# Two RWKV directions prepared side by side, and inverse roots taken on a few columns, in a two-layer mixer network

## The reference, cut to what matters

```python
kk = heads(k * k_k)
kk = kk * lax.rsqrt(jnp.sum(kk * kk, axis=-1, keepdims=True) + 1e-12)
for d in range(2):
    log_w = -jax.nn.softplus(-(w0[d] + jnp.tanh(wd) @ w2[d])) - 0.5
    decay = jnp.exp(-jnp.exp(log_w))
    a = jax.nn.sigmoid(a0[d] + ad @ a2[d])
    g = jax.nn.sigmoid(gd) @ g2[d]
    kd = heads(k * (1.0 + (a - 1.0) * k_a))
# S_t = S_{t-1}(diag(w_t) + z_t b_t^T) + v_t k_t^T, y_t = S_t r_t, in both directions
for (_, kd, _, g), yd in zip(per_dir, y_dirs):
    bonus = jnp.sum(rh * kd * r_k, axis=-1, keepdims=True) * vh
    outs.append((_head_norm(yd, gn_g, gn_b) + bonus) * g)
out = outs[0] + outs[1]
```

## Time and profile before

| | us |
|---|---|
| median of 3 runs | 3255.99 (3255.82 to 3256.31) |
| profiled execution, device time | 3254.52 |
| its span in the trace | 3252.7 |
| mean granted TensorE clock, share of full speed | 0.948 |

### The profile page before, as it was taken

How to read it: one execution, slowest core, us unless ns; L and a number is a source line. 1 busy time by engine, 2 the same in 40 slices (tenths; PEclk the granted TensorE clock), 3 DMA queues, 4 the chain that set the end, 5 groups by cost and what they waited for, 6 DMA issues and landing times. The chain is left out here.

```text
span 3252.7 us, 55368 instructions
## 1 busy us (share of the span) xinstructions
PE 2899.6 (89%) x23162; PEld 2478.3 (76%) x23162; DVE 2074.0 (64%) x2342; ACT 1553.3 (48%) x1802; POOL 44.2 (1%) x12
## 2 busy tenths in 40 slices
PE   6995796899998985968999999999999769997899
PEld 3872684799998853966877878778788649996799
DVE  2345655554445356656888888888888556665666
ACT  2234222443344242235766766767677434452553
POOL 0200000000000100000000000000000000000000
PEclk9997898999999997978999999999999889998999
DMA  6210464255454200007988989889799314542253
GB/s 264 104 65 7 157 223 144 77 182 181 168 187 162 91 33 1 4 1 294 368 309 309 372 307 351 321 306 371 307 348 372 133 52 156 182 169 80 108 191 117
DMA packets 86193, 616.02 MB, mean 189 GB/s; under 512 B 9592, under 2 KB 11264, under 8 KB 12032
## 3 DMA queue, kind: packets, MB, share of 16 engines
q1 hardware_dynamic: 82656, 601.92, 49.5%
q10 hardware_dynamic: 3360, 11.50, 1.0%
HBM read 612.33 MB, written 1.05 MB: 189 GB/s over the span
## 5 line engine op out<-in xcount | busy, mean ns | idle before, releaser
L2126 DVE TENSOR_TENSOR ring_split<-ring,arena_split 128x2048 fp32r<-128x2048 f32 x336 | 769.2, 2292 | 114.0 <-ACT arena_split L2056 103.1
L2056 ACT ACTIVATE arena_split<-ring 128x2048 fp32r<-128x2048 f32 x336 | 645.2, 1924 | 45.8 <-PE banks L1991 45.8
L305 DVE TENSOR_TENSOR ring_split<-ring,arena_split 128x2048 fp32r<-128x2048 f32 x174 | 405.4, 2332 | 360.1 <-ACT arena_split L299 360.1
L1970 PE MATMUL banks<-arena_split 128*128 128x512 f32 x1792 | 608.4, 402 | 11.6 <-DVE ring_split L2126 11.6
L1970 PEld LDWEIGHTS banks<-arena_split 128*128 128x128 f32 x1792 | 342.1, 191 | 87.7 <-DVE ring_split L2126 14.0
L299 ACT ACTIVATE arena_split<-ring 128x2048 fp32r<-128x2048 f32 x174 | 331.9, 1910 | 153.8 <-PE banks L971 54.7
L937 PE MATMUL banks<-mix_split,ring_split 128*128 128x256 f32 x1408 | 397.8, 283 | 0.0
L937 PE MATMUL banks<-mix_split,arena_split 128*128 128x256 f32 x1408 | 393.6, 280 | 2.0 <-DVE ring_split L305 1.6
L937 PE MATMUL banks<-h_split,arena_split 128*128 128x256 f32 x1408 | 395.1, 281 | 0.0
L1970 PE MATMUL banks<-ring_split,arena_split 128*128 128x512 f32 x896 | 356.5, 398 | 0.0
L636 PE MATMUL banks<-h_split,arena_split 128*128 128x256 f32 (+1 forms) x848 | 289.4, 341 | 59.4 <-DVE mix_split L452 59.4
(11 more groups left out here) (302 smaller groups left out, 4357.8 us busy)
## 6 DMA issues: line engine op xcount, KB each, us to landing
ring<-parts SPq DMA_DIRECT2D x574, 1024.0 KB, 4.8
arena<-bias ACTq DMA_DIRECT2D x2, 2048.0 KB, 8.9
x_buf<-xt ACTq DMA_DIRECT2D x1, 2048.0 KB, 23.9
constants<-con ACTq DMA_DIRECT2D x1, 2025.0 KB, 12.7
out<-x_buf ACTq DMA_DIRECT2D x1, 1024.0 KB, 4.8
arena<-lora ACTq DMA_DIRECT2D x2, 256.0 KB, 2.7
arena<-gate ACTq DMA_DIRECT2D x2, 256.0 KB, 2.9
arena<-sgw ACTq DMA_DIRECT2D x2, 256.0 KB
```

The lines of the kernel that those rows point to most:

```text
L305: dve.tensor_tensor(low_slots[:, n % RING, :], slots[:, n % RING, :], high[:, m % high.shape[1], :].bitcast(F32), ALU.subtract).then_inc(w ...
L1970: mm = pe.matmul(pair_bank(U), x[:, k, :], w[:, j, :], start=k == 0 and g == 0, stop=k == KT - 1 and g == 2)
L2056: act.activation(high[:, m % 3, :], slots[:, m % RING, :], ACT.Copy).then_inc(wh_ok.h, 1)
L2126: dve.tensor_tensor(low_slots[:, m % RING, :], slots[:, m % RING, :], high[:, m % 3, :].bitcast(F32), ALU.subtract).then_inc(wl_ok.h, 1)
```

## The change

In the preparation the head sums of `kk`, squared on DVE, are taken with the data as weights and two columns of `head_sum` as the moving operand: 128 tokens land on partitions, and the sums of 4 heads by 512 tokens are 16 columns. Root and inverse are taken on these 16 columns. PE puts the inverses back over each head's 64 features: a column, broadcast to 128x64, is the weight and the identity the moving operand (`over_head`). Both directions have buffers of their own, and ACT takes all sigmoids first (tanh as a sigmoid of twice the argument, with a DVE step behind it), then one root, then all exponentials. The factor on the log decays goes into the exponentials' scale; the exclusive decay is the inclusive one read a token earlier; the key scale runs on ACT. The bonus product is stored, and its head sum, the product with v and the gate stand behind the loop, on the needed tokens only. The layer norm of the convolution and the group norm take their inverse roots on few columns in the same way; the group norm goes q = 0, 2, 1, 3, with gain and gate fused into two DVE operations. Layer 1 leaves out the output half of `zr` and of its products for chunks that are not needed.

The diff, without the table of step names and most removed lines (they stand above):

```diff
...
+        head_cols = C("head_sum").rearrange("p (h f) -> p h f", h=2)[:, :, 0]
+        over_head = lambda a: a.broadcast_to((P, DH))
+        hs = [slice(0, DH), slice(DH, 2 * DH)]
...
+            pe.wait_ge(V_.h, V_.at("sq"))
+            for i in range(8):
+                hp, b = divmod(i, 4)
+                mm = pe.matmul(bank(7)[:, 2 * i:2 * i + 2], kd[:, hp, b * P:(b + 1) * P], head_cols, start=True, stop=True)
             mm.then_inc(P_.h, P_.one("kksum"))
...
+            pe.wait_ge(A_.h, A_.at("sw11"))
+            pe.wait_ge(V_.h, V_.at("inv"))
+            for i in range(8):
+                hp, b = divmod(i, 4)
+                for j, h in enumerate(hs):
+                    mm = pe.matmul(INV(hp)[h, b * P:(b + 1) * P], over_head(kk_inv[:, 2 * i + j:2 * i + j + 1]), C("ident"),
+                                   start=True, stop=True)
+            mm.then_inc(P_.h, P_.one("kkinv"))
...
+                act.activation(tw[0:64, d, :], us[0:64, 6 + 2 * d, :], ACT.Sigmoid, scale=2.0).then_inc(A_.h, A_.one(f"tanh{d}"))
+            for d in range(2):
+                act.activation(sgd[:, d, :], us[:, 7 + 2 * d, :], ACT.Sigmoid).then_inc(A_.h, A_.one(f"sgd{d}"))
...
+            def decays(d):
+                act.wait_ge(V_.h, V_.at(("scan10", "first")[d]))
+                act.activation(ep[d], en[d], ACT.Exp, scale=rate).then_inc(A_.h, A_.one(f"ep{d}"))
...
+                act.activation(en[d], en[d], ACT.Exp, scale=-rate).then_inc(A_.h, A_.one(f"en{d}"))
+            act.wait_ge(P_.h, P_.at("kksum"))
+            key_scale(0)
+            act.wait_ge(V_.h, V_.at("kkc"))
+            act.activation(kk_root, kk_root, ACT.Sqrt, bias=eps(EPS_KK)).then_inc(A_.h, A_.one("root"))
+            decays(0)
+            decays(1)
+            act.wait_ge(V_.h, V_.at("k0"))
+            key_scale(1)
...
+            own()
+            mult(kd, kk, kk, "sq")
+            for d in range(2):
+                dve.wait_ge(A_.h, A_.at(f"tanh{d}"))
+                dve.tensor_scalar(tw[0:64, d, :], tw[0:64, d, :], 2.0, -1.0, ALU.mult, ALU.add).then_inc(V_.h, V_.one(f"tw{d}"))
+            dve.wait_ge(P_.h, P_.at("kksum"))
+            dve.tensor_copy(kk_root, bank(7)[:, 0:16]).then_inc(V_.h, V_.one("kkc"))
+            for d in range(2):
...
+            own()
...
+            dve.wait_ge(A_.h, A_.at("root"))
+            dve.reciprocal(kk_inv, kk_root).then_inc(V_.h, V_.one("inv"))
+            def keys(d):
+                dve.wait_ge(A_.h, A_.at(f"ka1{d}"))
+                mult(kd, kd, k, f"kd{d}")
+                own()
+                for hp in range(2):
+                    dve.scalar_tensor_tensor(bonus[d][:, hp, c0:T], r[:, hp, c0:T], Q1(l, "r_k", hp), kd[:, hp, c0:T],
+                                             ALU.mult, ALU.mult).then_inc(V_.h, V_.one(f"rk{hp}{d}"))
+            def rows(d):
...
+                dve.wait_ge(P_.h, P_.at("kkinv"))
+                for hp in range(2):
+                    dve.scalar_tensor_tensor(zr[:, 2 * d + hp, :, 0, inner], e[:, hp, :, moved], -1.0, kc[:, hp, :, inner],
+                                             ALU.mult, ALU.mult).then_inc(V_.h, V_.one(f"z{hp}{d}"))
+                for hp in range(2):
+                    dve.tensor_scalar(zr[:, 2 * d + hp, :, 0, edge], kc[:, hp, :, edge], -1.0, None, ALU.mult)\
+                        .then_inc(V_.h, V_.one(f"e{hp}{d}"))
...
+            def columns(d):
+                own()
+                mult(bt[:, 2 * d:2 * d + 2, :], kk, av[d], f"b1{d}")
+                dve.wait_ge(A_.h, A_.at(f"en{d}"))
+                mult(kt[:, 2 * d:2 * d + 2, :], kd, en[d], f"k{d}")
+                own()
+                mult(bt[:, 2 * d:2 * d + 2, :], bt[:, 2 * d:2 * d + 2, :], en[d], f"b{d}")
             for d in range(2):
+                keys(d)
+                if not d:
+                    dve.wait_ge(P_.h, P_.at("kkinv"))
+                    for hp in range(2):
+                        mult(kk[:, hp, :], kk[:, hp, :], INV(hp), f"kkn{hp}")
+                    own()
+                rows(d)
+                columns(d)
...
+                    rows = 2 if seen(g) else 1
...
+                        mm = pe.matmul(bank(b)[h, q * 128:q * 128 + rows * CH], keys[h, q, c * CH:(c + 1) * CH], z_r[h],
...
+                if not j:
+                    for hp in range(2):
+                        mm = pe.matmul(bank(hp)[:, 0:n], C("head_sum"), bonus[0][:, hp, c0:T], start=True, stop=True)
+                    mm.then_inc(bnP.h, bnP.one("s0"))
+                    pe.matmul(bank(2)[:, 0:n], C("head_sum"), bonus[1][:, 0, c0:T], start=True, stop=True)\
+                        .then_inc(bnP.h, bnP.one("s1"))
                 fill_pe(pe, NG, f"u{j}")
...
+                if not j:
+                    pe.wait_ge(cvA.h, cvA.at("sq1"))
+                    for b in range(cv_n // P):
+                        for i in range(2):
+                            mm = pe.matmul(bank(4)[:, b:b + 1], cv_sq[:, i, b * P:(b + 1) * P], C("mean_cv")[:, 0:1],
...
+                    mm.then_inc(cvP.h, cvP.one("var"))
+                else:
+                    pe.wait_ge(cvV.h, cvV.at("inv"))
+                    for b in range(cv_n // P):
+                        mm = pe.matmul(bank(3)[:, b * P:(b + 1) * P], cv_inv[:, b:b + 1].broadcast_to((P, P)), C("ident"),
+                                       start=True, stop=True)
+                    mm.then_inc(cvP.h, cvP.one("inv"))
                 fill_pe(pe, NG, f"dx{j}")
...
+                    pe.wait_ge(bnV.h, bnV.at("v00"))
+                    pe.matmul(bank(0)[:, 0:n], C("head_sum"), bonus[1][:, 1, c0:T], start=True, stop=True)\
+                        .then_inc(bnP.h, bnP.one("s2"))
...
+                if j:
+                    dve.wait_ge(cvA.h, cvA.at("root"))
+                    dve.reciprocal(cv_inv[:, 0:cv_n // P], cv_root[:, 0:cv_n // P]).then_inc(cvV.h, cvV.one("inv"))
...
+                for hp in range(2):
+                    dve.wait_ge(bnP.h, bnP.at("s0" if not j else f"s{1 + hp}"))
...
+                    dve.tensor_tensor(bonus[j][:, hp, c0:T], sums, v[:, hp, c0:T], ALU.mult).then_inc(bnV.h, bnV.one(f"v{hp}{j}"))
+            dve.wait_ge(cvP.h, cvP.at("inv"))
...
+                dve.tensor_tensor(flat(acc[i]), flat(acc[i]), bank(3)[:, 0:cv_n], ALU.mult).then_inc(cvV.h, cvV.one(f"n{i}"))
...
+            dve.wait_ge(bnV.h, bnV.at("v11"))
+            for d in range(2):
+                for hp in range(2):
+                    o = bonus[d][:, hp, c0:T]
+                    dve.tensor_tensor(o, o, gg[:, 2 * d + hp, c0:T], ALU.mult).then_inc(bnV.h, bnV.one(f"g{hp}{d}"))
...
+            dve.tensor_tensor(bon[:, :, c0:T], bon[:, :, c0:T], bonus[1][:, :, c0:T], ALU.add).then_inc(bnV.h, bnV.one("add"))
...
+        order = (0, 2, 1, 3)
...
+            def var(q):
+                pe.wait_ge(A_.h, A_.at(f"s{q}"))
+                for b in range(nb):
+                    mm = pe.matmul(bank(4 + q)[:, 2 * b:2 * b + 2], sq[:, q, b * P:(b + 1) * P], head_cols, start=True, stop=True)
+                mm.then_inc(P_.h, P_.one(f"v{q}"))
+            def expand(q):
+                pe.wait_ge(V_.h, V_.at(f"i{q}"))
+                for b in range(nb):
+                    for j, h in enumerate(hs):
+                        mm = pe.matmul(bank(q)[h, b * P:(b + 1) * P], over_head(gn_inv[:, q, 2 * b + j:2 * b + j + 1]), C("ident"),
+                                       start=True, stop=True)
+                mm.then_inc(P_.h, P_.one(f"e{q}"))
...
+            for i in range(1, 4):
...
+            act.activation(warm, eps(EPS_RMS), ACT.Sqrt).then_inc(S("root_ready").h, S("root_ready").one())
...
+            for i in range(1, 4):
...
+            def invert(q):
+                dve.wait_ge(A_.h, A_.at(f"r{q}"))
+                dve.reciprocal(gn_inv[:, q, 0:2 * nb], gn_root[:, q, 0:2 * nb]).then_inc(V_.h, V_.one(f"i{q}"))
+            def gain(q):
+                dve.wait_ge(P_.h, P_.at(f"e{q}"))
+                dve.scalar_tensor_tensor(dv[:, q, :], dv[:, q, :], Q1(l, "gn_g", q % 2), bank(q)[:, 0:n], ALU.mult, ALU.mult)\
+                    .then_inc(V_.h, V_.one(f"g{q}"))
+            def gated(q):
+                own()
+                dve.scalar_tensor_tensor(dv[:, q, :], dv[:, q, :], Q1(l, "gn_b", q % 2), gg[:, q, c0:T], ALU.add, ALU.mult)\
+                    .then_inc(V_.h, V_.one(f"b{q}"))
...
+            invert(0)
+            own()
+                gain(hp)
+                invert(2 + hp)
+                gated(hp)
+                own()
+                dve.tensor_tensor(dv[:, hp, :], dv[:, hp, :], bon[:, hp, c0:T], ALU.add).then_inc(V_.h, V_.one(f"add{hp}"))
+                gain(2 + hp)
+                if not hp:
+                    invert(1)
+                gated(2 + hp)
+                own()
+                dve.tensor_tensor(mixT[:, 4 + hp, c0:T], dv[:, hp, :], dv[:, 2 + hp, :], ALU.add).then_inc(V_.h, V_.one(f"o{hp}"))
```

267 lines of the change are left out of this document (113 added, 154 removed).

## The result

The changed kernel takes 3183.7 us (median of four, 3179.3 to 3189.8) against 3255.9 for the kernel before (3254.5 to 3256.3): a ratio of 0.978, 95% interval 0.977 to 0.979. Five more executions beside later experiments gave 3182.4 against 3254.9, ratio 0.978 (0.976 to 0.979). The forecast was 3178, with 3168 to 3198 as the range. The profiled execution is the slowest of the four, 3189.8 us with a span of 3188.0; a second one, profiled later, took 3181.3 (span 3179.5).

What follows compares the result with a forecast made beforehand. PE was taken to bound most of the program, but DVE chains four stretches of 183 us. From 3254.5 us, savings in preparations, second loop and group norms less 5.8 lost gave 3176.4, with 1.5 to the median 3178; range 3168 to 3198.

Steps and rivals of the forecast that it cites:

- preparation, layer 0: Preparation of layer 0: a chain through DVE ending at 36.9 instead of 65.9 us, 29.0 us saved.
- preparation, layer 1: Preparation of layer 1: the same chain with half the tokens for r and bonus, 34.3 of 63.8 us, 29.5 saved.
- loop, layer 0: End of the first loop: last chunk 3.9 us later and 1.9 more on DVE behind it, 5.8 us lost.
- loop, layer 1: Second loop: fewer product columns and half masks save 2.8, its end loses 0.6 to 1; 2.2 us saved.
- group norm, layer 0: Group norm of layer 0: DVE-led behind the first expansion, 17.6 of 33.0 us, 15.4 saved.
- group norm, layer 1: Group norm of layer 1, half as wide: 12.5 of 20.3 us, 7.8 saved.
- rival 2: Each of the 160 expansion instructions pays its weight load: +9 to +17 us, about 3190; chance 0.06.
- rival 3: All 276 new small products run one by one, 0.33 us more each, 91 us: 3269; chance 0.02.
- Rival 4: Loop's end grows another 8 to 10 us as modulation pieces, ACT's copies and bonus wait in turn: 3187; chance 0.06.
- rival 1: PE's clock does not come up in preparations and group norms: about +18 us, 3196; chance 0.12.
- the first 5.3 us: Start of layer 0's group norm: mean products with the clock coming up, expected to stay at 5.3 us.
- DVE waits for no expansion after the first: Expected sign in the profile: group norms of 17.6 and 12.5 us, DVE waiting for no expansion but the first.

Runs made afterwards that it cites:

- experiment 2: Changed kernel with the key norms' inverse root back at full width, in DVE's idle gap ahead of the scans, without expansion: 3186.0 us (+3.6).
- experiment 6: Changed kernel with layer 1's key products against z and r back to both rows for every chunk: 3185.4 us (+2.9).
- Experiment 8: Changed kernel with products nobody reads put on PE where it idles, in the preparations and at the loop ends: 3169.4 us (-13.0).
- experiment 5: Changed kernel with the whole bonus term moved from the loop's end back into the preparation: 3183.9 us (+1.5).
- experiment 3: Changed kernel with the group norm alone back to wide sums, roots and inverses: 3202.3 us (+19.9).
- experiment 4: Changed kernel with the convolution's layer norm alone back to full width, without expansion: 3190.2 us (+7.8).
- experiment 1: The changed kernel again, with no edit: 3182.4 us (3181.3 to 3184.2).

## Why the prediction was right, and where its terms were off

By its own steps; the second profile stands behind the first, since the first has the dip:

| step | forecast | first profile | second |
|---|---|---|---|
| preparation, layer 0 | -29.0 | -27.30 | -27.70 |
| preparation, layer 1 | -29.5 | -28.85 | -28.85 |
| loop, layer 0 | +5.8 | +8.50 | +5.80 |
| loop, layer 1 | -2.2 | -1.80 | -1.95 |
| group norm, layer 0 | -15.4 | -12.85 | -13.25 |
| group norm, layer 1 | -7.8 | -7.20 | -7.00 |
| sum | -78.1 | -69.50 | -72.95 |

**The mechanism was right.** Four chains through DVE end where their phases end; 72.5 us between the medians stand against 73.0 in the windows of the second profile. The price of the expansion instructions, for which no row stood, holds: 16 in 1.09 us at full clock, 32 in 3.5 to 3.7 at half (0.055 and 0.107 apart beyond the finish of the last), so rivals 2 and 3 are out. The Trainium skill (TensorE: Matmul & The Clock Gate, Part 3: Packing small matmuls) lets a weight load overlap running products, in its list of what overlaps, only where the row group differs (its paragraph on the mechanism also allows a load into the background weight buffer); here every instruction uses all 128 rows, and the 0.055 and 0.107 leave no room for an exposed load. The trace disagrees with the rule of the list. The first out_project phase does not wait for weights: ACT starts it 0.2 us behind the group norm's end.

**The end of the first loop** is the term I had expected to be least sure, and in the second profile it is exact (+5.8; tail 28.4 against 22.8 before). Its two parts hold as well: from the mean product to the last chunk 4.2 us more (forecast 3.9), behind that 1.4 more (forecast 1.9). Rival 4, another 8 to 10 us, did not come. The first profile's +8.5 is 2.7 above the sum, by the dip of the clock and not by waits of PE, ACT and bonus for each other.

**What was mis-sized is the clock in short phases,** 4.9 us in all: rival 1 in a mild form. In the first preparation the low-rank products were to run at full clock after 4 us of work and did so after 8.8: 1.3 us in the phase. My 4 us came from a stretch with products of 512 columns only, and experiment 2, with such a head sum, needed 5. The step that failed is counting the 2-column head sum towards it in the same way. In the group norm I kept "the first 5.3 us"; they became 6.2 to 6.6, where the phase starts after 4.2 us of idle PE instead of 3.6, and its last expansions fell back to half clock, so the row "DVE waits for no expansion after the first" is wrong (0.5 and 0.6 us): 2.1 us. In the second group norm everything behind the means ran at half clock: 0.8. (That one has no fixed size: unaltered, it took 11.2 and 10.5 us in experiments 2 and 6, less than my 12.5.) The preparation of layer 1 lacks 0.7 for the same kind. Experiment 8 bears the clock out as the cause: it changes only what keeps PE busy, and these four windows are then 34.1, 33.2, 16.0 and 10.2 us, below my 36.9, 34.3, 17.6 and 12.5. It doesn't show that no smaller error of another kind hides in them.

**Two attributions inside a right sum were wrong.** I booked 6.6 us for the wide inverses; experiment 2 puts them back in another place for 0.3 and 1.0. And 12.7 for the bonus; experiment 5 shows 6.2 of it to be work that is merely done elsewhere. The removed sum was right because it was read from the whole phase, but neither number is what the edit is worth by itself. The group norm (20.8 us, experiment 3) and the convolution's layer norm (5.2 in windows, experiment 4) are worth what DVE's rows say, since nothing covers them.

What stays open: what causes the dip in the first loop's tail. It is in 8 of 12 profiles that have the products of one column there, and in neither of the two without them (the kernel before and experiment 4); but experiment 1 shows the same program without it, so that one profile of experiment 4 settles nothing. Open too is why the clock comes up early in the second group norm of some executions and not of others, behind the same end of the loop and the same idle time. Also open is the 4 us by which stages that no edit touches differ between executions, and what the waits marked "issue" in the loop's body are.

## What to carry to other kernels

A wide operation on DVE costs its row's time only where DVE ends the phase; before shrinking it, look for an idle gap ahead of the chain, and book per phase, not per instruction. Where a phase leaves PE idle for a few microseconds, price the next phase's products at both levels of the clock and take the lower one for its whole first stretch; bounds from a kernel with long products don't carry over. And if PE idles anyway, products that nobody reads can be worth more than the next rearrangement: here 13 us for three loops in the source.
